# Hybrid decoder trunk with top-4-of-32 experts on one core: down products of the experts as three fp32r passes instead of fp32 matmuls

## The chip, the cores and the metric

One core of a Trainium2 chip. The metric is the device time of one launch in microseconds, the median over runs of the same program; besides there is one profiled execution, whose own time stands in the table below.

## The reference

One layer for 1024 prompt tokens and 32 sample tokens (8 sequences of 4), model width 1024, all in fp32: conditioning and RMSNorm, an input projection, a recurrent head group (HGRN2) and a pooling group, an output projection with a residual, then the experts, a residual and a last RMSNorm. The change lies in the experts alone:

```python
def moe(h, w_router, b_router, w_gu, b_gu, w_down, b_down):   # top 4 of 32 experts, D_FF = 1024
    ...
    gu = lax.ragged_dot(xs, w_gu, group_sizes) + b_gu[e_sorted]
    gate = jnp.minimum(gu[:, :D_FF], SWIGLU_LIMIT)
    up = jnp.clip(gu[:, D_FF:], -SWIGLU_LIMIT, SWIGLU_LIMIT)
    act = gate * jax.nn.sigmoid(SWIGLU_ALPHA * gate) * (up + 1.0)
    out = lax.ragged_dot(act.astype(w_down.dtype), w_down, group_sizes) + b_down[e_sorted]
    out = out * probs.reshape(-1)[order][:, None].astype(out.dtype)
    y = jax.ops.segment_sum(out, tok_sorted, num_segments=n)
```

## The kernel before, in words

Four phases follow one another: `modulation`, `mixing` (with the router), `experts` and `combination`. The span spends 882 to 2496 us in `experts`, and only this function changes.

**Items.** The router leaves a table of items. An item is one expert with up to 128 of its tokens, and an item "with a tail" has up to 32 more (`TAIL`). Class 0 is plain, class 1 has a tail, class 2 is idle; `per_class` (L1398) walks the table on each engine in groups of eight and branches into `item(i, False)` or `item(i, True)`. Each item loads its expert's 12 MB anew.

**Weights.** SP loads an item's weights as 12 chunks of 1 MB into `raw0` to `raw11`: eight of gate and up (`KT` = 8 blocks of 128 rows of the model width, gate and up side by side) and four of down (`DN`, two blocks of 128 rows each). `reload` (L1433) waits until TensorE has used a chunk for the last time, by counting on `gu_done` (one per grain) or `dn_done` (one per pair of down blocks), and loads the next item's into the same place, in the order 0 to 11.

**Gate and up.** A grain is half of a gate-and-up chunk, 128 x 1024 numbers, 16 grains an item in the order of `ORDER`: first both halves of blocks 0 to 3, then the left halves of blocks 4 to 7, then the right ones. ACT rounds each grain to fp32r (`split_hi`, L1640), DVE subtracts that from the original (`split_lo`, L1708), into a ring of eight buffers `hi` and `lo` (`RING` = 8). TensorE computes hi x hi, hi x lo and lo x hi with the gathered rows, which are split in the same way (`xs`, by `rows_hi` and `rows_lo`): six matmuls of 128 x 512 a grain (L1592 to L1595), into the banks `pg[u][b]` (u: gate or up, b: half of the columns). The bias comes first, as a matmul of a selecting matrix with the biases (L1578). A grain's buffers are free for grain q + 8 when `gu_done` has counted grain q.

**SwiGLU.** `swiglu(i, b)` (L1717) on DVE takes half b: gate (min), up (clip), then with ACT's sigmoid (`squash`, L1651) the product and `act1`. b = 0 may start when grains 0 to 11 are done, b = 1 after all 16.

**Down.** TensorE transposes each half of `act1` (`transpose_act`, L1522) into the bank `pt0`, ACT copies it to `aT` (`act_cols`, L1655), and the 16 down matmuls (L1529, 8 blocks x 2 halves of the output) run in fp32 straight from `raw8` to `raw11`. Between them TensorE transposes the second half of `act1` (before block 2) and the next item's gathered rows (`transpose_rows`: the first half ahead of the down stage, the second before block 3).

**Output.** ACT copies bank `py0` and DVE copies `py1` to `y` (L1692, L1773), and POOL scatters `y` with an add to the output rows in DRAM (L1502). Then POOL gathers the rows for the next item. `y_out` counts landings of the scatters.

**Tail.** In an item with a tail TensorE also runs the 32 rows in fp32 from the raw chunks: `tail_up` (32 matmuls with `TAILED` at grains 6 and 11) into `py0`, `swiglu_tail` on DVE, and `tail_down` (four matmuls of 128 x 256 for each of eight blocks) into the bank `pg[1][0]`, two blocks at a time ahead of down blocks 0, 2, 4 and 6. ACT copies that bank to `act1` (L1688), POOL scatters it (L1497). Each engine's order is written out in its own `item` (TensorE L1563, ACT L1659, DVE L1752, POOL L1484). ACT's order after `squash(i, 0)` is: three grains of the next item, `act_cols(0)`, `squash(1)`, `rows_hi(0)`, one grain, `act_cols(1)`, `rows_hi(1)`, four grains, the tail's copies, the copy of `y`. DVE's is the same with `lo`, and ends with `select` (the next item's selecting matrix) and its copy of `y`. Before each item's first copy and before its first sigmoid ACT loads a function table.

## Time and profile before

| | us |
|---|---|
| median of 3 runs | 2581.58 |
| lowest, highest | 2580.42, 2586.19 |
| the profiled execution, its own time | 2580.96 |
| its span, first to last instruction | 2579.4 |
| TensorE (PE) busy in the span | 2373.8 |
| DVE, ACT, POOL busy | 1391.8, 1117.1, 566.2 |

Busy times come from the profiled execution. Matmuls are pipelined: a matmul's recorded length runs into the next one, so the pace is read from start to start. An fp32 matmul stands in the trace as two records, an fp32r matmul as one.

### The profile page before, as it was taken

To read this page: it belongs to the slowest core of one execution; us is meant where nothing else is said; L and a number is where in the kernel's file an instruction comes from. 1 tells how busy PE (TensorE), PEld (TensorE's weight loads), DVE (VectorE), ACT (ScalarE), POOL (GpSimd) and SP (SyncE) were. 2 spreads that over 40 slices of the span, in tenths; PEclk is the share of its full clock that TensorE was granted. 3 is DMA by queue.
4 is the path that set the end of the run, shared out by engine and by line. 5 is a ranking of instruction groups with operands and counts; after the bars stand their busy time and mean duration, and the time that the engine had idled before them with its cause. 6 is when DMAs were issued, how large, how long until landed. Compare 5 with 4: busy or idle time off the path is not lost. (4 is left out here: it accounts for less than half of the span.)

```text
span 2579.4 us, 36293 instructions
## 1 busy us (share of the span) xinstructions
PE 2373.8 (92%) x11130; PEld 1553.7 (60%) x11131; DVE 1391.8 (54%) x1996; ACT 1117.1 (43%) x1443; POOL 566.2 (22%) x843
## 2 busy tenths in 40 slices
PE   8589999999986399999999999999999999999965
PEld 1177677777754256556567566766575666676641
DVE  0124554545333566556466666766565575766647
ACT  0023333333221345445455455555454554555532
POOL 0122333333211312112112121221121212121110
PEclk9799999999687699999999999999999999999985
DMA  8840000000020787778689889988797797999945
GB/s 307 330 173 34 33 33 33 27 14 23 29 66 12 290 320 286 264 277 318 251 313 344 312 319 371 343 317 313 293 335 301 258 362 277 350 343 368 350 161 222
DMA packets 142977, 604.43 MB, mean 234 GB/s; under 512 B 20129, under 2 KB 25262, under 8 KB 104470
## 3 DMA queue, kind: packets, MB, share of 16 engines
q1 hardware_dynamic: 120311, 551.51, 55.0%
q0 software_dynamic: 21968, 50.99, 8.1%
q10 hardware_dynamic: 662, 1.50, 0.2%
q8 instruction: 18, 0.29, 0.0%
q14 instruction: 18, 0.14, 0.0%
HBM read 561.82 MB, written 42.30 MB: 234 GB/s over the span
## 5 line engine op out<-in xcount | busy, mean ns | idle before, releaser
L1710 DVE TENSOR_TENSOR lo<-raw,hi 128x1024 fp32r<-128x1024 f32 x600 | 716.6, 1222 | 200.1 <-ACT hi L1645 173.2
L1645 ACT ACTIVATE hi<-raw 128x1024 fp32r<-128x1024 f32 x600 | 613.1, 1054 | 172.4 <-PE pg L1595 172.4
L1529 PE MATMUL py<-raw,aT 128*128 128x512 f32 x1184 | 537.9, 599 | 6.3 <-ACT aT L1657 6.3
L1592 PE MATMUL pg<-hi,xs 128*128 128x512 f32 x1184 | 467.3, 395 | 0.0
L1593 PE MATMUL pg<-lo,xs 128*128 128x512 f32 x1184 | 465.3, 393 | 0.0
L1595 PE MATMUL pg<-hi,xs 128*128 128x512 f32 x1184 | 367.3, 392 | 0.0
L1529 PEld LDWEIGHTS py<-raw,aT 128*128 128x128 f32 x1184 | 214.5, 190 | 250.2 <-issue 238.0
L1592 PEld LDWEIGHTS pg<-hi,xs 128*128 128x128 f32 x1184 | 222.9, 188 | 68.9 <-issue 20.1
L1595 PEld LDWEIGHTS pg<-hi,xs 128*128 128x128 f32 x1184 | 222.8, 188 | 49.2
L1593 PEld LDWEIGHTS pg<-lo,xs 128*128 128x128 f32 x1184 | 223.1, 188 | 47.4
L392 PE MATMUL X<-hT,w_in 128*128 128x128 f32 (+1 forms) x1728 | 223.8, 289 | 0.8 <-issue 0.8
L392 PEld LDWEIGHTS X<-hT,w_in 128*128 128x128 f32 x1728 | 219.2, 208 | 1.2 <-issue 1.2
L1502 POOL DMA_INDIRECT moe_rows<-y,now x37 | 61.3, 1657 | 631.3 <-DVE y L1773 631.3
L498 PE MATMUL X<-w_out,mixT 128*128 128x512 f32 (+1 forms) x288 | 130.8, 614 | 7.1 <-issue 6.8
L400 PE MATMUL X<-w_in,hT 128*128 128x512 f32 (+1 forms) x288 | 128.2, 604 | 6.1 <-ACT vx L637 6.1
L1714 DVE TENSOR_TENSOR xs<-pt,xs 128x512 fp32r<-128x512 f32 x76 | 52.2, 687 | 118.5 <-ACT xs L1649 118.5
L1497 POOL DMA_INDIRECT moe_rows<-actm,now_t x12 | 17.2, 1435 | 433.5 <-ACT actm L1688 433.5
L1657 ACT ACTIVATE aT<-pt 128x512 f32<-128x512 f32 x74 | 44.2, 598 | 150.5 <-PE pt L1525 150.5
L498 PEld LDWEIGHTS X<-w_out,mixT 128*128 128x128 f32 (+1 forms) x288 | 52.9, 186 | 79.7 <-issue 79.2
L1653 ACT ACTIVATE sigm<-gatem 128x512 f32<-128x512 f32 x74 | 46.5, 629 | 124.1 <-DVE gatem L1724 124.1
L1724 DVE TENSOR_SCALAR gatem<-pg 128x512 f32<-128x512 f32 x74 | 51.1, 690 | 87.3 <-PE pg L1595 83.2
L400 PEld LDWEIGHTS X<-w_in,hT 128*128 128x128 f32 (+1 forms) x288 | 52.5, 185 | 75.2 <-issue 68.3
(295 smaller groups left out, 2581.0 us busy)
## 6 DMA issues: line engine op xcount, KB each, us to landing
raw<-in_w_gu SPq DMA_DIRECT2D x300, 1024.0 KB, 7.3
raw<-in_w_down SPq DMA_DIRECT2D x148, 1024.0 KB, 6.9
wada<-in_w_ada SPq DMA_DIRECT2D x12, 2048.0 KB, 7.7
w_in<-in_w_in SPq DMA_DIRECT2D x5, 2048.0 KB, 14.1
moe_rows<-zero SPq DMA_DIRECT2D x9, 512.0 KB, 11.6
x<-in_x_prompt SPq DMA_DIRECT2D x8, 512.0 KB
w_out<-in_w_out SPq DMA_DIRECT2D x1, 4096.0 KB, 25.0
xr<-in_x_prompt SPq DMA_DIRECT2D x8, 512.0 KB, 3.7
```

Source lines behind the costliest of these rows:

```text
L392: last = pe.matmul(bank[:, m * T:(m + 1) * T], w_in[:, kt, first + m * P:first + (m + 1) * P], hT[:, kt * T:(kt + 1) * T], start=(kt == 0) ...
L400: last = pe.matmul(bank[0:T, :], hT[:, kt * T:(kt + 1) * T], w_in[:, kt, first:first + HW], start=(kt == 0), stop=(kt == KT - 1))
L498: last = pe.matmul(bank[0:T, :], mixT[:, kt * T:(kt + 1) * T], w_out[:, kt, n * 512:(n + 1) * 512], start=(kt == 0), stop=(kt == KT - 1))
L1502: pool.indirect_dma_start(scratch["acc"][:, :], bass.IndirectOffsetOnAxis(ap=now[:, 1:2], axis=0), y[:, :], None, compute_op=ALU.add).then ...
L1529: return pe.matmul(py[n][:, :], aT[:, kt, :], raw[KT + kt // 2][:, kt % 2, n * 512:(n + 1) * 512], start=(kt == 0), stop=(kt == KT - 1))
L1592: pe.matmul(pg[u][b][:, :], xs[:, kt, 0, :], wh[:, u, :], start=False, stop=False)
L1593: pe.matmul(pg[u][b][:, :], xs[:, kt, 0, :], wl[:, u, :], start=False, stop=False)
L1595: last = pe.matmul(pg[u][b][:, :], xs[:, kt, 1, :], wh[:, u, :], start=False, stop=(kt == KT - 1))
L1645: act.activation(hi[q % RING][:, :, :], grain(q), ACT.Copy).then_inc(s["hi"], 1)
L1710: dve.tensor_tensor(lo[q % RING][:, :, :], grain(q), hi[q % RING][:, :, :].bitcast(F32), ALU.subtract).then_inc(s["lo"], 1)
L1714: dve.tensor_tensor(xs[:, half * 4:half * 4 + 4, 1, :], pt[1][:, :].rearrange("p (k t) -> p k t", k=4), xs[:, half * 4:half * 4 + 4, 0, :] ...
L1724: dve.tensor_scalar(gate[:, :], pg[0][b][:, :], LIMIT, None, ALU.min).then_inc(s["gate"], 1)
```

## The change

- **Down in three passes.** `GRAINS` becomes 24: grain 16 + kt is down block kt, and ACT and DVE split these eight grains as they do those of gate and up. `aT` gets a second plane: ACT writes the rounded activations, a new `act_lo` on DVE writes the rest (reads the bank `pt0`). `down_hi` and `down_lo` issue six fp32r matmuls a block instead of two fp32 ones. All consumers count on one semaphore `used` (23 a item, and `y_mm1` as the 24th).
- **Orders.** ACT and DVE convert grains 8 to 18 ahead of the first swiglu, 19 and 20 behind it, `act_lo(0)` ahead of `swiglu(1)`, grains 21 and 22 ahead of the second half's copy and `act_lo(1)`, 23 behind the rows, then the next item's 0 to 7. `select` moves ahead of grain 23.
- **Output.** ACT copies both halves of y, last in its item. DVE copies none. y is `act1`.
- **Tail.** `tail_down` runs four blocks at a time ahead of down blocks 0 and 4, and `yt_mm` is signalled at the second. ACT copies the bank to `pair` (which also holds `gate` and `up`) ahead of the next item's eight grains.
- **Spark.** Each item on ACT begins with a Sigmoid of a single number.

```diff
-    GRAINS, RING = 2 * KT, 8
+    GU, GRAINS, RING = 2 * KT, 3 * KT, 8
...
-        gate, sig, up = (sb(n, [P, 512]) for n in ("gatem", "sigm", "upm"))
+        sig, pair = sb("sigm", [P, 512]), sb("pair", [P, FF])
+        gate, up = pair[:, 0:512], pair[:, 512:1024]
         act1 = sb("actm", [P, FF])
-        aT = sb("aT", [P, FT, P])
-        y = sb("y", [P, D])
+        aT = sb("aT", [P, FT, 2, P], F32R)
+        y = act1
...
+        def wait_used(eng, i, q):
+
+            if q < GRAINS - 1:
+                eng.wait_ge(s["used"], i * (GRAINS - 1) + q + 1)
+            else:
+                eng.wait_ge(s["y_mm1"], i + 1)
...
-            def down(i, kt, n):
-                return pe.matmul(py[n][:, :], aT[:, kt, :], raw[KT + kt // 2][:, kt % 2, n * 512:(n + 1) * 512],
-                                 start=(kt == 0), stop=(kt == KT - 1))
+            def down_hi(kt, n):
+                q = GU + kt
+                pe.matmul(py[n][:, :], aT[:, kt, 0, :], hi[q % RING][:, n, :], start=(kt == 0), stop=False)
+                pe.matmul(py[n][:, :], aT[:, kt, 0, :], lo[q % RING][:, n, :], start=False, stop=False)
+
+            def down_lo(kt, n):
+                return pe.matmul(py[n][:, :], aT[:, kt, 1, :], hi[(GU + kt) % RING][:, n, :], start=False, stop=(kt == KT - 1))
...
-                    if tail and kt % 2 == 0:
+                    if tail and kt % 4 == 0:
                         if kt == 0:
                             pe.wait_ge(s["aT_t"], i + 1)
-                        tail_down(kt)
-                        tail_down(kt + 1)
+                        for c in range(2):
+                            pe.wait_ge(s[f"raw{KT + kt // 2 + c}"], i * 16 + 16)
+                        for k in range(4):
+                            last = tail_down(kt + k)
+                        if kt:
+                            last.then_inc(s["yt_mm"], 1)
+                    pe.wait_ge(s["lo"], i * GRAINS + GU + kt + 1)
                     for n in range(2):
-                        last = down(i, kt, n)
-                    if kt % 2:
-                        last.then_inc(s["dn_done"], 1)
+                        down_hi(kt, n)
+                    if kt % 4 == 0:
+                        pe.wait_ge(s["alo"], i * 2 + kt // 4 + 1)
+                    for n in range(2):
+                        last = down_lo(kt, n)
+                    last.then_inc(s["used"], 1)
+                pe.wait_ge(s["lo"], i * GRAINS + GRAINS)
                 for n in range(2):
                     for kt in (KT - 2, KT - 1):
-                        last = down(i, kt, n)
+                        down_hi(kt, n)
+                        last = down_lo(kt, n)
+                        if n and kt == KT - 2:
+                            last.then_inc(s["used"], 1)
                     last.then_inc(s[f"y_mm{n}"], 1)
...
             def item(i, tail):
+                act.activation(spark[:, 1:2], spark[:, 0:1], ACT.Sigmoid)
...
-                for q in range(RING, GRAINS):
+                for q in range(RING, GU + 3):
                     split_hi(i, q)
...
                 squash(i, 0)
-                for q in range(3):
-                    split_hi(i, GRAINS + q)
+                for q in range(GU + 3, GU + 5):
+                    split_hi(i, q)
                 act_cols(i, 0)
...
                 squash(i, 1)
                 rows_hi(i + 1, 0)
-                split_hi(i, GRAINS + 3)
+                split_hi(i, GU + 5)
+                split_hi(i, GU + 6)
                 act_cols(i, 1)
                 rows_hi(i + 1, 1)
-                for q in range(4, RING):
-                    split_hi(i, GRAINS + q)
+                split_hi(i, GU + 7)
                 if tail:
                     act.wait_ge(s["yt_mm"], i + 1)
                     for n in range(4):
-                        last = act.activation(act1[0:TAIL, n * W:(n + 1) * W], pg[1][0][n * TAIL:(n + 1) * TAIL, 0:W], ACT.Copy)
+                        last = act.activation(pair[0:TAIL, n * W:(n + 1) * W], pg[1][0][n * TAIL:(n + 1) * TAIL, 0:W], ACT.Copy)
                     last.then_inc(s["y_t"], 1)
+                for q in range(RING):
+                    split_hi(i, GRAINS + q)
                 act.wait_ge(s["y_mm0"], i + 1)
                 act.wait_ge(s["y_out"], i * 32 + 32)
                 act.activation(y[:, 0:512], py[0][:, :], ACT.Copy).then_inc(s["y0"], 1)
-
+                act.wait_ge(s["y_mm1"], i + 1)
+                act.activation(y[:, 512:1024], py[1][:, :], ACT.Copy).then_inc(s["y1"], 1)
...
+            def act_lo(i, b):
+                dve.wait_ge(s["aT"], i * 2 + b + 1)
+                dve.tensor_tensor(aT[:, b * 4:b * 4 + 4, 1, :], pt[0][:, :].rearrange("p (k t) -> p k t", k=4),
+                                  aT[:, b * 4:b * 4 + 4, 0, :].bitcast(F32), ALU.subtract).then_inc(s["alo"], 1)
...
                 swiglu(i, 0)
-                for q in range(2):
-                    split_lo(i, GRAINS + q)
+                for q in range(GU + 3, GU + 5):
+                    split_lo(i, q)
+                act_lo(i, 0)
                 swiglu(i, 1)
                 rows_lo(i + 1, 0)
-                split_lo(i, GRAINS + 2)
-                split_lo(i, GRAINS + 3)
+                split_lo(i, GU + 5)
+                split_lo(i, GU + 6)
+                act_lo(i, 1)
                 rows_lo(i + 1, 1)
-                for q in range(4, RING):
+                select(i + 1)
+                split_lo(i, GU + 7)
+                for q in range(RING):
                     split_lo(i, GRAINS + q)
-                select(i + 1)
-                dve.wait_ge(s["y_mm1"], i + 1)
-                dve.wait_ge(s["y_out"], i * 32 + 32)
-                dve.tensor_copy(y[:, 512:1024], py[1][:, :]).then_inc(s["y1"], 1)
```

## Rows read from the trace of the kernel before

**Rows 1.** Stretches: length, each engine's busy us, granted clock, DMA share, GB/s.
```profile
1213.57:1266.69 53.12, 52.72 (x296) 30.82 (x294) 28.14 (x32) 25.23 (x32) 8.56 (x13) 1.00 0.74 276
1567.58:1606.53 38.95, 38.70 (x150) 26.52 (x149) 26.56 (x28) 22.66 (x25) 8.14 (x12) 1.00 0.93 352
```

**Rows 2.** Stretches again, POOL's busy us in the tail's scatter (L1497) alone.
```profile
976.33:1015.28 38.95, 0.85 (x1) 1.00 0.90 337
...
2183.57:2222.51 38.94, 0.85 (x1) 1.00 0.90 336
```

**Rows 3.** Groups: count | busy us, mean ns | idle before, releaser.
```profile
L1529 PE MATMUL py<-raw,aT 128*128 128x512 f32 x1184 | 537.9, 599 | 6.3 <-ACT aT L1657 6.3
...
L1502 POOL DMA_INDIRECT moe_rows<-y,now x37 | 61.3, 1657 | 631.3 <-DVE y L1773 631.3
...
L1645 ACT ACT_TABLE_LOAD x25 | 32.1, 1283 | 19.9 <-issue 19.9
...
L1497 POOL DMA_INDIRECT moe_rows<-actm,now_t x12 | 17.2, 1435 | 433.5 <-ACT actm L1688 433.5
```

**Rows 4.** PE in order of time, plain item: start us, us, line, tile, count.
```profile
1514.36 3.70 PE L1529 MATMUL py<-raw,aT 128*128 128x512 f32 x8 [0.25 <-ACT aT L1657]
1517.89 0.60 PE L1525 MATMUL pt<-ident,actm 128*128 128x128 f32 x4
1518.33 1.88 PE L1529 MATMUL py<-raw,aT 128*128 128x512 f32 x4
1520.05 0.60 PE L1519 MATMUL pt<-ident,xg 128*128 128x128 f32 x4
...
1528.67 1.02 PE L1578 MATMUL pg<-bgu,sel 128*128 128x512 f32 x2
1529.53 0.39 PE L1592 MATMUL pg<-hi,xs 128*128 128x512 f32 x1
...
1530.91 0.62 PE L1578 MATMUL pg<-bgu,sel 128*128 128x512 f32 x2
```

**Rows 5.** DVE in order of time, the same item.
```profile
1507.97 0.69 DVE L1724 TENSOR_SCALAR gatem<-pg 128x512 f32<-128x512 f32 x1 [3.37 <-PE pg L1595]
...
1510.24 0.69 DVE L1732 SCALAR_TENSOR_TENSOR actm<-upm,gatem 128x512 f32<-128x512 f32 x1
1510.85 2.35 DVE L1710 TENSOR_TENSOR lo<-raw,hi 128x1024 fp32r<-128x1024 f32 x2
...
1522.26 4.63 DVE L1710 TENSOR_TENSOR lo<-raw,hi 128x1024 fp32r<-128x1024 f32 x4 [0.25 <-ACT hi L1645]
...
1529.27 0.69 DVE L1773 COPY y<-py 128x512 f32<-128x512 f32 x1 [2.25 <-PE py L1529]
```

**Rows 6.** ACT in order of time, the same item.
```profile
1520.69 0.60 ACT L1649 ACTIVATE xs<-pt 128x512 fp32r<-128x512 f32 x1 [1.56 <-PE pt L1519]
1521.18 3.88 ACT L1645 ACTIVATE hi<-raw 128x1024 fp32r<-128x1024 f32 x4
...
1529.03 1.28 ACT L1645 ACT_TABLE_LOAD   x1 [0.79 <-issue]
1531.11 1.06 ACT L1645 ACTIVATE hi<-raw 128x1024 fp32r<-128x1024 f32 x1 [0.80 <-PE pg L1595]
```

**Rows 7.** PE in order of time, an item with a tail.
```profile
1247.79 1.07 PE L1559 MATMUL pg<-raw,xs_t 128*32 128x256 f32 x16 [0.40 <-ACT xs_t L1677]
1248.79 3.70 PE L1529 MATMUL py<-raw,aT 128*128 128x512 f32 x8
...
1267.19 0.68 PE L1536 MATMUL pt<-ident,xg_t 32*128 32x32 f32 x8
```

**Rows 8.** ACT in order of time, the end of that item.
```profile
1263.69 1.54 ACT L1688 ACTIVATE actm<-pg 32x256 f32<-32x256 f32 x4 [3.00 <-PE pg L1559]
...
1267.88 1.28 ACT L1662 ACT_TABLE_LOAD   x1 [1.62 <-issue]
1269.17 0.38 ACT L1662 ACTIVATE xs_t<-pt 128x256 f32<-128x256 f32 x1
```

More of the change, by code:

```diff
@@ L1363, in experts @@
         idx = sb("idx", [P, 3], I32)
+        spark = sb("spark", [1, 2])
         nxt = sb("nxt", [P, 3], I32)
@@ L1408, in per_class, with chunk @@
                                 body(i, True)
+        def chunk(q):
+            return ORDER[q][0] if q < GU else KT + (q - GU) // 2
         def grain(q):
-            kt, b = ORDER[q % GRAINS]
-            return raw[kt][:, :, b * 512:(b + 1) * 512]
+            if q < GU:
+                return raw[chunk(q)][:, :, ORDER[q][1] * 512:(ORDER[q][1] + 1) * 512]
+            return raw[chunk(q)][:, q % 2, :].rearrange("p (u n) -> p u n", u=2)
+        def wait_used(eng, i, q):
[3 more added lines that the diff above has]
+                eng.wait_ge(s["y_mm1"], i + 1)
         @block.sync
@@ L1497, in item @@
                     pool.indirect_dma_start(scratch["acc"][:, :], bass.IndirectOffsetOnAxis(ap=now_t[0:TAIL, 1:2], axis=0),
-                                            act1[0:TAIL, :], None, compute_op=ALU.add).then_inc(s["y_out"], 16)
+                                            pair[0:TAIL, :], None, compute_op=ALU.add).then_inc(s["y_out"], 16)
                 pool.wait_ge(s["y0"], i + 2)
@@ L1640, in split_hi @@
             def split_hi(i, q):
-                kt, b = ORDER[q % GRAINS]
-                act.wait_ge(s[f"raw{kt}"], (i + q // GRAINS) * 16 + 16)
+                act.wait_ge(s[f"raw{chunk(q % GRAINS)}"], (i + q // GRAINS) * 16 + 16)
                 if q >= RING:
-                    act.wait_ge(s["gu_done"], i * GRAINS + q - RING + 1)
-                act.activation(hi[q % RING][:, :, :], grain(q), ACT.Copy).then_inc(s["hi"], 1)
+                    wait_used(act, i, q - RING)
+                act.activation(hi[q % RING][:, :, :], grain(q % GRAINS), ACT.Copy).then_inc(s["hi"], 1)
             def rows_hi(item, half):
@@ L1656, in act_cols @@
                 act.wait_ge(s["aT_ps"], i * 2 + b + 1)
-                act.activation(aT[:, b * 4:b * 4 + 4, :], pt[0][:, :].rearrange("p (k t) -> p k t", k=4), ACT.Copy).then_inc(s["aT"], 1)
+                act.activation(aT[:, b * 4:b * 4 + 4, 0, :], pt[0][:, :].rearrange("p (k t) -> p k t", k=4), ACT.Copy).then_inc(s["aT"], 1)
             def item(i, tail):
+                act.activation(spark[:, 1:2], spark[:, 0:1], ACT.Sigmoid)
                 if tail:
@@ L1692, in item @@
                 act.activation(y[:, 0:512], py[0][:, :], ACT.Copy).then_inc(s["y0"], 1)
+                act.wait_ge(s["y_mm1"], i + 1)
+                act.activation(y[:, 512:1024], py[1][:, :], ACT.Copy).then_inc(s["y1"], 1)
+            act.wait_ge(s["spark"], 1)
             act.sem_inc(s["y0"], 1)
@@ L1717, in swiglu @@
             def swiglu(i, b):
[L1718 removed]
+                wait_used(dve, i, (GU - 4 if b == 0 else GU) - 1)
                 if b:
@@ L1752, in item @@
             def item(i, tail):
-                for q in range(RING, GRAINS):
+                for q in range(RING, GU + 3):
                     split_lo(i, q)
```

21 lines of the change are left out of this document (7 added, 14 removed).

## The prediction

> **What bounds the kernel now.** I read the page first, for the share of each engine, then the stretches of the expert stage item by item, then the costliest groups, and last the order in time of one plain item and one item with a tail. TensorE is busy for 2373.8 of 2579.4 us, the others for little over half or less (table above). In a plain item it is busy 38.70 of 38.95 us, at the full granted clock of 1.00, while DVE has 26.56 and ACT 22.66 us and the DMA engines are busy for 0.93 of the time; an item with a tail takes 53.12 us [rows 1]. So each item is as long as TensorE's own list of matmuls, and the other engines follow. There are 37 items (scatters of y) and 12 of them have a tail (scatters of the tail, [rows 3]); 24 are plain, and the first one is plain and starts behind the router; 8 of the 24 plain ones follow a tail (their stretch begins with the rest of the tail's scatter; first and last of the 8 in [rows 2]), 16 follow a plain one.
>
> What the reader is to see in the plain item: the down stage goes from 1514.36 to 1528.67 [rows 4]. The bias pair that follows holds 0.86 us up to grain 0, though six matmuls of a grain take only 1.38 us with the next bias pair at 1530.91, 0.23 us each; so two need 0.46, and the down stage really ends 0.40 us later, at 1529.07. It takes 14.71 us: 32 records (two per fp32 matmul, x1184 in [rows 3] over 37 items), two groups of four transposes at 0.44 us (1517.89 to 1518.33), and 0.1 us at the start. That is 0.43 us a record, 0.86 us a matmul, 13.73 us for the 16.
>
> **TensorE's part of the change.** Each fp32 down matmul becomes three fp32r ones of the kind that grains of gate and up use: 3 x 0.23 = 0.69 us in place of 0.86. Eight chunks of six matmuls take 8 x 1.38 = 11.04 us instead of 13.73: 2.69 us less per item if nothing waits. By the Trainium skill (TensorE: Matmul & The Clock Gate, section "Wait — 56ns, not 53.3ns?") warm matmuls of 512 columns start 215.7 ns apart, which as an estimate makes three of them 0.65 us and the gain about 0.76 us an item larger; the rows show 0.23 us for this kernel's pattern, so the page's value is not used.
>
> Items with a tail: from the first tail_down to the end 1247.79 to 1267.19, plus the same 0.40, is 19.80 us [rows 7]. Known parts: 4 x 1.0 for eight tail_downs (1247.79 to 1248.79), 13.73, and 0.88 for transposes, 18.61; the other 1.19 lie in the nine changes from one kind of matmul to another, 0.13 each. After: 4.0 + 11.04 + 0.88 + five changes x 0.13 = 16.57. That is 3.2 us less.
>
> **A new wait in plain items.** act_lo(0), a 128x512 operation out of PSUM like the gate's 0.69 us [rows 5], stands on DVE ahead of swiglu(1), and swiglu(1) is what transpose_act(1) waits for. Call A the start of act_lo(0), which is when TensorE starts the down stage. The next DVE operation begins 0.60 us on (1510.24, 0.69 long, next at 1510.85); swiglu takes 2.96 us from its gate to the end of act (1507.97 to 1510.93): transpose_act(1) at A + 3.65 with 0.1 to pick it up. TensorE has done two chunks by A + 2.8, so it stands for 0.8 us. Then 0.44, one chunk, 0.44 and five chunks: end at A + 3.65 + 0.88 + 6 x 1.38 = A + 12.81, against 14.71 before: 1.90 us less, not 2.69. The wait for act_lo(0) itself costs nothing, four matmuls of chunk 0 (0.92 us) cover it. With a tail, four tail_downs (2.0 us) lie ahead of chunk 0 and cover the whole of this wait.
>
> **Does the conversion keep up?** ACT and DVE now convert 24 grains instead of 16. The old items leave both idle; the new order leaves little. The chain around one plain item, from A:
> - rows transposes at 3.65 + 0.44 + 1.38 = 5.47; rows_hi(1) 0.64 later (1520.05 to 1520.69, [rows 4, 6]): 6.11. hi of grain 23 0.49 later: 6.60. Grains come 0.945 us apart (3.88 for four, one is 1.06 long, [rows 6]): the last of the eight for the next item, 31, starts at 14.16.
> - The two output copies, now both on ACT (DVE's copy of 0.69 is gone): starts at 15.11 and 15.6, end 16.2. A table load of 1.28, spark 0.2, next hi (grain 8) 17.75 to 18.8.
> - DVE: 11 grains at 1.14 (4.63 for four less 2.35 for two, [rows 5]), 12.5; swiglu(0) 2.88; two grains 2.3: next act_lo(0) at 36.5.
> TensorE's own ring gives end 12.81 plus what it needs from a real end to the next down stage, 38.94 - 14.71 = 24.23: 37.04. So TensorE stays the bound, with only 0.5 us to spare, and a plain item takes 37.04.
>
> Three unknowns lie in that chain. The spark is priced between 0 and 0.38 (the 256-column activation, [rows 8]); that one and the 512-column one of 0.60 differ by 0.22, which leaves about 0.2 without columns. The branch code between items left ACT idle 0.79 us before the load [rows 6]; I take nothing, because ACT's instruction stream would be ahead of its engine there, with the bound 0.79. The table load comes twice per plain item now, at the first copy (x25 in [rows 3]) and again at the sigmoid, which needs a set of its own. The spark asks for the Sigmoid set first, so I take one load; bound, two, 1.28 more.
> What follows a load: the row at 1269.17 starts 0.01 us after the load of 1267.88 ends [rows 8], so I take nothing more. The Trainium skill (ScalarE: Activation LUTs, section "What ACT_TABLE_LOAD costs") adds about 1380 ns of drain to the 1283 ns of the load. The trace agrees with the load and shows no such drain here.
>
> After a tail the chain is later: ACT copies the tail's output when the last tail_down is through, 0.13 us to pick up and 4 x 0.39 (1.54 for four, [rows 8]), and only then starts the eight grains: the last starts 1.68 + 6.62 = 8.3 after it, TensorE ends 4 x 1.38 + 0.13 = 5.65 after it. So hi 31 is at end + 2.65, the next act_lo(0) at end + 2.65 + (36.5 - 14.16) = end + 25.0 instead of 24.23. The item after a tail takes 37.8: 1.1 us less than before.
>
> **At no cost.** DVE's three grains more ahead of a tail's swiglu (3.4 us) are covered by the 20 fp32 tail_up matmuls that TensorE does before grain 11. The transfers: 0.93 x 38.95 = 36.2 us of DMA work per plain item, just under 37.04. SP's reloads follow the same matmuls as before, in the same order. Down chunks are now wanted eight grains (11 us) sooner, by ACT. The first of them is the ninth in SP's order; chunk 0 is released seven grains in (10.9 us with the biases), a chunk of 1.05 MB takes 3.0 us at the 352 GB/s of [rows 1], so it has landed at 38 us, and ACT wants it after the next item's grain 8, at 37 + 13. If that cover goes, the item is as long as the DMA work. POOL's scatter of y moves 2.5 us later, behind ACT's copies; swiglu(0) awaits its landing, 12 grains (16.5 us) into the item, and the gather queued behind it on POOL serves transposes 16 grains in. The tail's scatter moves earlier, since its copy no longer stands behind eight grains (7.6 us); TensorE's next item needs that bank, and it is copied 4 us before the item ends. y now shares act1, and gate and up share the tile that the tail's scatter reads; both are guarded by the same landing, so by the same 16.5 us. The clock: TensorE waits 0.25 us for aT [rows 4] and 0.40 us for aT_t [rows 7] now, and the granted clock stays at 1.00 [rows 1]; I take it that 0.8 us do not change that.
>
> **Sum.** 16 x 1.90 = 30.4; 8 x 1.1 = 8.8; 12 x 3.2 = 38.4; first item 1.9; the last output copy ends 16.2 - 12.81 = 3.4 us after TensorE instead of 0.9 (1529.96 less 1529.07), so -2.5. Together 77.0. The profiled execution took 2580.96 us (span 2579.4), which gives 2504.0; the median of the runs is 0.6 higher: 2504.6, say 2505.
>
> **Rivals.**
> 1. The conversion chain sets the pace (23%). A second table load (the spark does not do what it is for), or the 0.79 us of branches plus a dearer spark, add 1.3 to 1.4 us to a chain with 0.5 to spare: plain items 37.9, those after a tail 39.2. Sum 16 x 1.0 - 8 x 0.3 + 38.4 + 1.9 - 2.5 - 1.4 = 50: 2531. For it: the small margin, and DVE's sum of busy time. Against: the instruction stream can run ahead. The drain that the page on ScalarE states would give this same time of 2531.
> 2. TensorE does not wait (10%): every item gives its full 2.69 or 3.2, sum about 102, 2479. It needs swiglu(1) to come 0.8 us sooner than my order gives; its floor is the DMA work of 36.2, which it just touches.
> 3. Slower (5%): the transfers become the bound. Place: ACT's hi of a grain waits for its raw chunk. The engines are 0.93 busy, and the same 12 chunks plus gathers and an accumulating scatter must go through in a shorter item. It decides the sign where DMA work per plain item passes 40.5 us, because 24 x 1.6 eats the 38 of the tails; at 41 us the sum is 24 x 2.06 - 38.4 + 0.6 = +12: 2593. Against: bytes are the same, and 36.2 would have to grow by 12%.
> 4. Everything else, among it no change (2%).
>
> **How the numbers follow.** Forecast 60%, with 2495 to 2515 as its own range. The range goes from 2484, which holds part of the way to rival 2, to 2535, which holds rival 1; about 15% lies outside. Faster 0.93, within 0.2% (5 us, about what a measurement of this kernel can tell) 0.02, slower 0.05.
>
> **What would show it.** Plain items of 37.0 and items with a tail of 49.9; TensorE idle 0.8 us before transpose_act(1), put down to DVE's act; down matmuls 0.23 us apart; one table load per item, at the spark; ACT's next-item hi following the load at once. Wrong, if hi or lo of down grains wait for DMA, if act_lo(0) starts later than the copy of aT (the chain is then the bound), or if the granted clock leaves 1.00 in the expert stage.

## The result, and the profile after

The kernel after the change takes **2524.9 us** (median of 4 runs, 2524.7 to 2527.4) where the one before took 2581.8 on the same chip: a ratio of 0.978, with a 95% interval of 0.976 to 0.980 (the ratios below have theirs in brackets). The forecast case came true, inside the range, but 20 us above the predicted 2505. The profiled execution took 2524.7 us, its span is 2523.1. TensorE is busy for 2293.3 us, DVE for 1726.9 and ACT for 1364.2.

First the stretches, as in [rows 1]: length, each engine's busy us, granted clock, DMA share, GB/s. They are item 15, plain behind a plain one, and item 7, with a tail.

```profile
1544.61:1582.11 37.50, 36.71 (x165) 29.30 (x164) 35.49 (x38) 29.35 (x35) 11.60 (x12) 1.00 0.99 373
1205.17:1255.64 50.47, 49.86 (x311) 34.08 (x310) 36.81 (x41) 30.76 (x41) 11.23 (x13) 1.00 0.81 293
```

The plain item is 1.4 us shorter. TensorE (36.71 us busy), DVE (35.49) and the DMA queues (a share of 0.99) are now near its length of 37.50, and ACT has 29.35. Item lengths below are always from the start of an item's last down matmul to that of the next:

| us | before | predicted | after |
|---|---|---|---|
| plain after plain (16 items) | 38.93 | 37.04 | 37.51 |
| plain after a tail (8) | 38.93 | 37.8 | 37.74 |
| with a tail (11 of 12) | 53.12 | 49.9 | 50.48 |
| item 1, the first with a tail | 53.21 | 49.9 | 55.83 |
| first item (gain) | | 1.9 | 1.9 |
| end of the last item to the end of the span | 84.4 | 86.9 | 87.5 |

TensorE in order of time, end of item 15, after the change (start us, us, line, tile, count, idle before):

```profile
1566.28 0.63 PE L1610 MATMUL pg<-hi,xs 128*128 128x512 f32 x2
...
1567.68 0.63 PE L1610 MATMUL pg<-hi,xs 128*128 128x512 f32 x2
1568.14 0.60 PE L1536 MATMUL pt<-ident,actm 128*128 128x128 f32 x4
1568.58 0.60 PE L1530 MATMUL pt<-ident,xg 128*128 128x128 f32 x4
1569.51 0.49 PE L1541 MATMUL py<-hi,aT 128*128 128x512 f32 x1 [0.33 <-ACT aT L1677]
...
1571.94 0.62 PE L1545 MATMUL py<-hi,aT 128*128 128x512 f32 x2
1573.02 0.66 PE L1536 MATMUL pt<-ident,actm 128*128 128x128 f32 x4 [0.47 <-DVE actm L1758]
```

DVE in the same item, to be read beside [rows 5]:

```profile
1566.45 2.35 DVE L1736 TENSOR_TENSOR lo<-raw,hi 128x1024 fp32r<-128x1024 f32 x2
1569.41 0.69 DVE L1777 TENSOR_TENSOR aT<-pt,aT 128x512 fp32r<-128x512 f32 x1 [0.60 <-ACT aT L1677]
1570.02 0.68 DVE L1750 TENSOR_SCALAR pair<-pg 128x512 f32<-128x512 f32 x1
...
1572.28 0.69 DVE L1758 SCALAR_TENSOR_TENSOR actm<-pair 128x512 f32<-128x512 f32 x1
```

The new wait is where it was foretold: two chunks of the down stage, then TensorE stands until DVE has written the second half of act, 3.61 us behind the start of `act_lo(0)` (1569.41 to 1573.02; predicted 3.65). DVE had to wait 0.60 us for the copy of aT, so after a plain item the conversion chain (ACT's rounding and DVE's subtracting, one grain behind the other) is not the bound. ACT at the end of the item and over its border, beside [rows 6]:

```profile
1576.05 8.63 ACT L1665 ACTIVATE hi<-raw 128x1024 fp32r<-128x1024 f32 x9
1584.58 0.58 ACT L1715 ACTIVATE actm<-py 128x512 f32<-128x512 f32 x1
1585.05 0.59 ACT L1717 ACTIVATE actm<-py 128x512 f32<-128x512 f32 x1
1585.66 1.28 ACT L1680 ACT_TABLE_LOAD   x1
1586.96 0.20 ACT L1680 ACTIVATE spark<-spark 1x1 f32<-1x1 f32 x1
1587.07 1.04 ACT L1665 ACTIVATE hi<-raw 128x1024 fp32r<-128x1024 f32 x1
```

No gap for branches ahead of the load, none behind it, and a spark of 0.20 us: the three unknowns of the chain came out at their chosen values. The groups have one load at the spark per item, 37 in all.

### The profile page after: what moved, and what is told of

Read it like the earlier page. It is cut to its first block and busy times, and to the rows that moved or that the text cites. A ratio compares the mean times of both kernels' runs of the same rounds, so it can differ in the third digit from the quotient of the medians.

```text
span 2523.1 us, 38969 instructions
## 1 busy us (share of the span) xinstructions
PE 2293.3 (91%) x11722; PEld 1665.6 (66%) x11723; DVE 1726.9 (68%) x2330; ACT 1364.2 (54%) x1776; POOL 666.7 (26%) x843
## 5 line engine op out<-in xcount | busy, mean ns | idle before, releaser
L1736 DVE TENSOR_TENSOR lo<-raw,hi 128x1024 fp32r<-128x1024 f32 x896 | 1039.4, 1218 | 123.1 <-ACT hi L1665 121.3
L1665 ACT ACTIVATE hi<-raw 128x1024 fp32r<-128x1024 f32 x896 | 887.0, 1049 | 103.9 <-PE pg L1610 103.5
L1541 PE MATMUL py<-hi,aT 128*128 128x512 f32 x592 | 244.6, 413 | 8.2 <-ACT aT L1677 7.8
L1513 POOL DMA_INDIRECT moe_rows<-actm,now x37 | 88.7, 2398 | 585.3 <-ACT actm L1717 585.3
L1542 PE MATMUL py<-lo,aT 128*128 128x512 f32 x592 | 233.9, 395 | 0.0
L1545 PE MATMUL py<-hi,aT 128*128 128x512 f32 x592 | 197.7, 394 | 0.0
L1541 PEld LDWEIGHTS py<-hi,aT 128*128 128x128 f32 x592 | 111.1, 188 | 45.0 <-issue 18.3
L1545 PEld LDWEIGHTS py<-hi,aT 128*128 128x128 f32 x592 | 110.7, 187 | 27.3
L1542 PEld LDWEIGHTS py<-lo,aT 128*128 128x128 f32 x592 | 111.4, 188 | 21.3
L1673 ACT ACTIVATE sigm<-pair 128x512 f32<-128x512 f32 x74 | 46.8, 632 | 125.5 <-DVE pair L1750 125.5
L1508 POOL DMA_INDIRECT moe_rows<-pair,now_t x12 | 17.2, 1435 | 346.2 <-ACT pair L1709 346.2
```

The lines of the kernel that those rows point to most:

```text
L1513: pool.indirect_dma_start(scratch["acc"][:, :], bass.IndirectOffsetOnAxis(ap=now[:, 1:2], axis=0), y[:, :], None, compute_op=ALU.add).then ...
L1541: pe.matmul(py[n][:, :], aT[:, kt, 0, :], hi[q % RING][:, n, :], start=(kt == 0), stop=False)
L1542: pe.matmul(py[n][:, :], aT[:, kt, 0, :], lo[q % RING][:, n, :], start=False, stop=False)
L1545: return pe.matmul(py[n][:, :], aT[:, kt, 1, :], hi[(GU + kt) % RING][:, n, :], start=False, stop=(kt == KT - 1))
L1665: act.activation(hi[q % RING][:, :, :], grain(q % GRAINS), ACT.Copy).then_inc(s["hi"], 1)
L1736: dve.tensor_tensor(lo[q % RING][:, :, :], grain(q % GRAINS), hi[q % RING][:, :, :].bitcast(F32), ALU.subtract).then_inc(s["lo"], 1)
```

## The experiments

### What slowed the matmuls

In the rows of TensorE above two grains are 1.40 us apart (1566.28, 1567.68). Before the change they were 1.37, as these two rows of the kernel before show, from the middle of an item:

```profile
1541.91 0.62 PE L1595 MATMUL pg<-hi,xs 128*128 128x512 f32 x2
1543.29 0.62 PE L1595 MATMUL pg<-hi,xs 128*128 128x512 f32 x2
```

Over all items an fp32r matmul of 512 columns takes 0.2292 us before and 0.2333 after, from start to start (the pace, below). With 148 of them an item (96 of the grains, four of the biases, 48 of the down stage) this makes 0.6 us: the excess of the tail items (50.48 over 49.9), and more than that of the plain ones (0.47), where the wait for act came out 0.18 shorter than reckoned. The pace is the same whether DVE and ACT are busy or not, and fp32 matmuls stay at 0.429 a record. What else had changed was the place of the operands in SBUF. Tiles are put one behind the other, and the 8 bytes of `spark` take up 32. `xs` lay at byte 202176 of each partition before and at 202208 after, an odd multiple of 64 before and of 32 after. `aT`, the stationary operand of the down matmuls, is at an odd multiple of 32 after, too. `hi` and `lo` lie at multiples of 128 in both.

**e1_spark64**: the changed kernel, with `spark` 64 bytes long, which puts `xs` and `aT` at multiples of 128.

```diff
-        spark = sb("spark", [1, 2])
+        spark = sb("spark", [1, 16])
```

> The changed kernel with one size altered: the tile spark has 16 numbers instead of 2, so that every tile allocated behind it (xs and aT among them, from which the stationary operand is loaded) lies 32 bytes further on and at a multiple of 64 again, as xs did before the change. In the changed kernel fp32r matmuls start 0.2333 us apart against 0.2292 in the kernel before, whether or not DVE and ACT are busy beside them. Theory 'placement': the pace goes back to 0.229, plain items after a plain one from 37.51 to 37.1, items with a tail from 50.48 to 50.0, items after a tail stay near 37.7 (ACT's chain), total about 2512. Rival 'load' (more conversions beside the matmuls, or a longer program, slow them): the pace stays 0.233 and the total 2525.

Measured: 2503.5 us, ratio 0.970 (0.969 to 0.971), and a pace of 0.227, better than the 0.229 expected; e8 below asks why. Items of 36.75 (plain behind plain), 37.70 (plain behind a tail) and 49.77 us (with a tail); item lengths are given in this order from here on. The grains are 1.36 apart (two rows of TensorE):

```profile
1553.88 0.62 PE L1610 MATMUL pg<-hi,xs 128*128 128x512 f32 x2
1555.24 0.62 PE L1610 MATMUL pg<-hi,xs 128*128 128x512 f32 x2
```

**e2_before_pad32**: the converse, the kernel before with `xs` pushed on by 32 bytes.

```diff
+        gap = sb("gap", [1, 2])
         nxt = sb("nxt", [P, 3], I32)
```

> The kernel before with an unused tile of 8 bytes in the place where the changed kernel has spark: xs lies 32 bytes on, at an odd multiple of 32; hi, lo and the raw chunks stay. Theory 'placement': the pace of fp32r matmuls goes from 0.2292 to 0.233; 96 of them and 4 bias matmuls an item, x 0.0041 = 0.4 us, x 37 = 15 us: about 2597. Rival 'load': nothing changes, 2582.

Measured: 2594.5 us, 1.005 (1.0035 to 1.006); plain items 39.31, items with a tail 53.49, pace 0.2333.

**e3_before_ring_pad32**: the kernel before with the rings `hi` and `lo` at odd multiples of 32 and `xs` not (64 bytes on, it is at a multiple of 128).

```diff
+        gap = sb("gap", [1, 2])
         hi = [sb(f"hi{j}"
...
+        gap2 = sb("gap2", [1, 2])
         table = sb("table", [1, (ITEMS + 2) * 3], I32)
```

> The kernel before with an unused tile of 8 bytes ahead of the ring hi and lo, and another behind it: the moving operands hi and lo lie 32 bytes on, at odd multiples of 32, and xs lies 64 bytes on, at a multiple of 64. Theory 'placement, of the stationary operand only': 2582, pace 0.229. 'Placement, of either operand': about 2597. 'Load': 2582 here and in the run with the pad ahead of xs.

Measured: 2595.8 us, 1.005 (1.004 to 1.007), items 39.31 and 53.47, pace 0.233. Either operand alone costs the whole of it.

**e8_before_pad64**: the kernel before with `xs` at a multiple of 128 (`gap` of 64 bytes).

> The kernel before with an unused tile of 64 bytes ahead of xs. In the kernel before xs lies at an odd multiple of 64, in the changed kernel with the 64-byte spark at a multiple of 128, and the pace is 0.229 in the one and 0.227 in the other. Theory 'multiples of 128 are better still': the pace goes to 0.227, 100 matmuls an item x 0.002 x 37 = 7 us: about 2574. Rival 'the pace of 0.227 came with something else': 2582.

Measured: 2572.7 us, 0.997 (0.996 to 0.998), items 38.74 and 52.93, pace 0.227.

So the change without the shift is seen twice: at odd multiples of 32 it takes 2594.5 to 2524.9, at multiples of 128 it takes 2572.7 to 2503.5, 69.6 and 69.2 us. In the kernel before, `xs` at an odd multiple of 32 instead of 64 costs 12.7 (2594.5 less 2581.8).

### The spark

**e4_no_spark**: the changed kernel without it.

```diff
-                act.activation(spark[:, 1:2], spark[:, 0:1], ACT.Sigmoid)
```

> The changed kernel without the spark (the Sigmoid of one number at the start of each item on ACT). If the spark saves a table load, ACT loads a table twice per item again: at the first copy, which delays the next item's grain 8 by nothing new (the load stands there either way, the spark's 0.2 us go), and again before squash(0), behind grain 18, where ACT waits 1.9 us for DVE in a plain item anyway. Theory 'hidden': the second load fits in that wait, the total stays within 3 us of 2525, and items after a tail get 0.1 to 0.2 us shorter. Rival 'on the chain' (my rival 1 of the prediction): the load of 1.28 us delays squash(0), swiglu(0) and act_lo(0); with 0.6 us of slack at act_lo(0) in plain items and none after a tail, +0.5 us in 16 and +1.1 us in 8 items: 2540.

Measured: 2525.0 us, 0.978 (the same ratio as with it), items of 37.50, 37.67 and 50.48. Each plain item has two loads now, at its first copy and at the sigmoid (groups of ACT):

```profile
L1665 ACT ACT_TABLE_LOAD x25 | 32.1, 1283 | 0.4
L1673 ACT ACT_TABLE_LOAD x25 | 32.1, 1283 | 0.5
```

After a plain item the chain has the room for a second load; after a tail, where the chain is the bound, nothing is lost either. The spark is worth nothing here, and the second load of my rival 1 would not have cost what I gave it.

### The place of the tail's copies

**e6_tail_copy_late**: the changed kernel with ACT's copies of the tail's bank behind the next item's eight grains again, as before the change.

```diff
+                for q in range(RING):
+                    split_hi(i, GRAINS + q)
                 if tail:
                     act.wait_ge(s["yt_mm"], i + 1)
...
-                for q in range(RING):
-                    split_hi(i, GRAINS + q)
```

> The changed kernel with ACT's copies of the tail's bank put back behind the next item's eight hi grains. The last of these grains waits for y_mm1, the end of the down stage, so y_t comes after it: H31 + 0.95 + 1.55, with H31 starting 1.1 us sooner without the copies, at about the end + 1.1; TensorE's next bias waits for y_t. Theory 'TensorE waits': about 3.7 us at the start of each item after a tail, and a stretch of the low clock behind it where the wait is that long: 12 x 3.7 = 44 less what the next item gets back, total 2560 to 2575. Rival 'hidden': 2525.

Measured: 2581.3 us, 1.000 (0.999 to 1.001). The twelve items behind a tail grow from 37.7 to 42.7 and from 50.5 to 54.6 us on average, and of the others only item 1 does, by 0.7. That is more than the 2560 to 2575 us expected. TensorE at the border of items 8 and 9, and the stretches from that border (columns as above):

```profile
1327.20 0.39 PE L1545 MATMUL py<-hi,aT 128*128 128x512 f32 x1
1330.92 0.71 PE L1593 MATMUL pg<-bgu,sel 128*128 128x512 f32 x2 [3.32 <-issue]
...
1334.20 0.63 PE L1607 MATMUL pg<-hi,xs 128*128 128x512 f32 x1
1334.62 0.63 PE L1608 MATMUL pg<-lo,xs 128*128 128x512 f32 x1
```
```profile
1327.40:1331.00 3.60, 0.28 (x2) 0.12 (x2) 3.10 (x3) 3.54 (x8) 0.00 (x0) 1.00 1.01 398
1331.00:1340.00 9.00, 9.00 (x33) 7.15 (x34) 3.50 (x3) 5.88 (x7) 6.03 (x5) 0.81 0.79 184
```

and ACT:

```profile
1326.93 2.00 ACT L1665 ACTIVATE hi<-raw 128x1024 fp32r<-128x1024 f32 x2 [1.04 <-PE py L1545]
1328.85 1.52 ACT L1711 ACTIVATE pair<-pg 32x256 f32<-32x256 f32 x4
```

The bank is the next item's first one for `up`; it is free at 1330.37 (1328.85 + 1.52), and TensorE had been done since 1327.4. Its next matmul starts 0.55 us after that. The profile names no releaser, so that the bank is the cause rests on this edit. The wait has a second part: behind it the granted clock is 0.81 on average over 9 us, and the matmuls are 0.42 apart for a while instead of 0.23. With three passes instead of fp32, and the copies where they were, the kernel is no faster than before: the place of the copies is as much a part of the gain as the passes. The prediction had this right but at no more than a clause ("copied 4 us before the item ends").

### The shared y, and POOL

**e7_y1_on_dve**: the changed kernel, with the second copy of y back on DVE, behind its eight grains.

```diff
-                act.wait_ge(s["y_mm1"], i + 1)
-                act.activation(y[:, 512:1024], py[1][:, :], ACT.Copy).then_inc(s["y1"], 1)
...
                 for q in range(RING):
                     split_lo(i, GRAINS + q)
+                dve.wait_ge(s["y_mm1"], i + 1)
+                dve.wait_ge(s["y_out"], i * 32 + 32)
+                dve.tensor_copy(y[:, 512:1024], py[1][:, :]).then_inc(s["y1"], 1)
```

> The changed kernel with the copy of the second half of y back on DVE, behind the next item's eight lo grains and ahead of its grain 8. ACT's table load and grain 8 come 0.5 us sooner. DVE ends its eight grains 5.3 us into the item and starts grain 8 at 6.0 (plain) with a gap of 0.66, so the copy (0.69) replaces the gap. Theory 'DVE's sum is what counts after a tail': items after a tail keep 37.7 or gain up to 0.3, plain ones 37.5; total 2523 to 2526; the end of the kernel is later by up to 1 us. Rival 'ACT's chain counts': items after a tail 0.5 us shorter, total 2521.

Measured: 2629.2 us, 1.019 (1.017 to 1.020), far over what I expected. Plain items behind plain ones take 43.3 to 44.4 us. All others are as in the changed kernel or a little shorter (37.51 and 50.51), but for item 1 (56.75). The scatter is issued 6.8 us into an item instead of 4.4. In item 11 DVE and then POOL:

```profile
1392.45 10.39 DVE L1734 TENSOR_TENSOR lo<-raw,hi 128x1024 fp32r<-128x1024 f32 x9
1403.01 1.23 DVE L1734 TENSOR_TENSOR lo<-raw,hi 128x1024 fp32r<-128x1024 f32 x1 [0.17 <-ACT hi L1665]
...
1412.32 0.69 DVE L1748 TENSOR_SCALAR pair<-pg 128x512 f32<-128x512 f32 x1 [6.68 <-DMA moe_rows<-actm,now]
```
```profile
1393.39 9.77 POOL L1513 DMA_INDIRECT moe_rows<-actm,now  x1 [14.73 <-DVE actm L1806]
```

POOL's scatter instruction takes 9.77 us instead of 1.66 [rows 3], and ends at 1403.16, 0.3 us after DVE has paused for the first time (1402.84). One subtraction earlier, at 1401.61, DVE had begun 1.22 us behind the one before instead of 1.135; POOL ends 1.55 us behind that. `swiglu(0)` waits for the landing, because y is `act1` now.

**e5_reorder**: e1 with an order that does away with the wait of the down stage: `swiglu(1)` ahead of `act_lo(0)`, the two passes with `aT`'s first plane for blocks 0 to 3, both transposes, then the third passes; the second half is transposed into the free bank `pg[0][1]`.

```diff
                     for n in range(2):
                         down_hi(kt, n)
-                    if kt % 4 == 0:
+                    if kt < 3:
+                        continue
+                    if kt == 3:
+                        transpose_act(i, 1)
+                        transpose_rows(i + 1, 1)
+                    if kt <= 4:
                         pe.wait_ge(s["alo"], i * 2 + kt // 4 + 1)
...
+                    for k in range(4) if kt == 3 else (kt,):
...
-                act_lo(i, 0)
                 swiglu(i, 1)
+                act_lo(i, 0)
```

> The changed kernel with the 64-byte spark and another order around the down stage: DVE runs swiglu(1) ahead of act_lo(0); TensorE runs the hi and lo passes of down blocks 0 to 3 first (16 matmuls), then transpose_act(1) and the second transposes of rows, then the four blocks' third passes; the second half's transposes go to the bank pg[0][1], which is free by then. Theory 'the wait for act is a stall that the order makes': TensorE's idle time ahead of transpose_act(1) (0.5 us between records, 13.5 in all in the changed kernel) goes. In plain items after a plain one the conversion chain of ACT and DVE is then the bound at 36.4 (it was 36.75), after a tail 36.2 to 36.5 (it was 37.7), because swiglu(1) and with it the whole of DVE's list no longer stands behind the copy of aT; total about 2486. Rival 'the conversion chain was the bound everywhere already': no more than 3 us under the 2503 of the run with the 64-byte spark.

Measured: 2542.9 us, 0.986 (0.984 to 0.987), though most items got shorter: 36.01, 36.94 and 49.71. Five plain items, each the second behind a tail, took 45 to 48.6. The waits of DVE say where (waited for: us in total, times, longest):

```profile
DVE pair L1752 <- DMA moe_rows<-actm,now: 52.9, 5, 11.9
```

POOL in item 10, one of the five, and DVE over the same time:

```profile
1340.07 16.16 POOL L1513 DMA_INDIRECT moe_rows<-actm,now  x1 [16.88 <-ACT actm L1719]
```
```profile
1333.03 21.66 DVE L1738 TENSOR_TENSOR lo<-raw,hi 128x1024 fp32r<-128x1024 f32 x19
1366.59 0.69 DVE L1752 TENSOR_SCALAR pair<-pg 128x512 f32<-128x512 f32 x1 [11.90 <-DMA moe_rows<-actm,now]
```

DVE subtracts 19 times without a pause, until 1354.69, and POOL's instruction ends at 1356.23. (Three more scatters took 10.5 us in items with a tail, which did not get longer.) In item 11, where DVE has a pause of 0.65 us at 1389.7, it took 2.54 us. Two theories were left: DVE's unbroken run holds POOL up, or the scatter comes at a bad time for the queues, which at 36 us an item have no rest. Four kernels on this:

**e9_y_early** and **e10_reorder_y_early**: e1 and e5 with ACT's two copies of y ahead of its last three grains, so that the scatter is issued sooner: 1.9 us into a plain item instead of 4.5 in e1 and 4.1 in e5.

```diff
-                for q in range(RING):
+                for q in range(RING - 3):
                     split_hi(i, GRAINS + q)
...
                 act.activation(y[:, 512:1024], py[1][:, :], ACT.Copy).then_inc(s["y1"], 1)
+                for q in range(RING - 3, RING):
+                    split_hi(i, GRAINS + q)
```

> The kernel with spark at 64 bytes (2503.5 us), with ACT's two copies of y placed ahead of the last three hi grains (after the copies of grains 24 to 28) instead of behind all of them. The scatter is then issued about two grains (2.7 us) sooner. If the scatter's landing is hidden in that kernel, the 36 inner items do not change (36.75, 37.7 and 49.8 us) and only the last item gains, by at most 2.7 us: 2500.5 to 2503.5. If the three last hi copies, pushed back by the y copies (some 1.9 us), reach TensorE's first matmuls of the next item, items get longer by up to 1 us each and the kernel gets slower than 2503.5.

Measured: 2501.2 us, 0.969 (0.968 to 0.971), items as in e1: only the end of the kernel gained (88.0 us behind the last item's last down matmul in e1, 84.2 here). POOL and DVE in item 11 hold something against the first theory in its plain form:

```profile
1371.48 10.30 DVE L1738 TENSOR_TENSOR lo<-raw,hi 128x1024 fp32r<-128x1024 f32 x9
```
```profile
1378.14 1.78 POOL L1513 DMA_INDIRECT moe_rows<-actm,now  x1 [20.21 <-ACT actm L1717]
```

Here POOL's instruction takes 1.78 us in the middle of nine subtractions without a pause, and so it does in 25 of the 37 items.

> The reordered kernel (2542.9 us, whose five plain items of 45 to 48.6 us come with scatters that land 15 to 26 us after issue), with the same early copies of y. Theory one: the scatter's work on POOL is held up by DVE's unbroken run of subtractions, so issued 2.7 us sooner it gets through ahead of that run; landings fall back to 7 or 8 us, no item is over 40 us, items are 36.0, 36.9 and 49.7 us, and the kernel takes about 2483 us. Theory two: the queues fall behind because items of 36.0 us are shorter than the transfers of an item need; then the time of the scatter's issue does not matter, the five long items stay, and the kernel takes about 2540 us.

Measured: **2486.5 us**, 0.963 (0.962 to 0.9645), with no item over 37 among the plain ones: 36.0 mostly, 36.95 and 49.71. That is the best of all kernels here, 38 us below the one after the change. POOL in item 11, and DVE:

```profile
1374.50 5.66 POOL L1513 DMA_INDIRECT moe_rows<-actm,now  x1 [14.80 <-ACT actm L1719]
```
```profile
1369.44 9.16 DVE L1740 TENSOR_TENSOR lo<-raw,hi 128x1024 fp32r<-128x1024 f32 x8
1378.98 12.57 DVE L1740 TENSOR_TENSOR lo<-raw,hi 128x1024 fp32r<-128x1024 f32 x11 [0.37 <-ACT hi L1667]
```

The instruction is issued while DVE runs eight grains and gets through at the pause of 0.37 us ahead of the next eleven: not ahead of DVE's run, as expected, but in a break of it, and the landing takes about 11 us rather than 7 or 8. In item 10 of e5 there was no break for 14.6 us behind the issue.

**e11_reorder_dve_pause** and **e12_y1_dve_pause**: e5 and e7 with nothing sooner, but DVE waits at the head of an item until POOL is through.

```diff
                                         y[:, :], None, compute_op=ALU.add).then_inc(s["y_out"], 16 if tail else 32)
+                pool.engine_nop().then_inc(s["gone"], 1)
...
             def item(i, tail):
+                dve.wait_ge(s["gone"], i + 1)
                 for q in range(RING, GU + 3):
                     split_lo(i, q)
```

> The reordered kernel of 2542.9 us with its scatter as late as it was (issued 4.1 us into an item), but DVE waits at the head of each item until POOL is through its scatter instruction. In that kernel's item 10 the scatter instruction lasted 16.2 us and ended 1.5 us after a run of 17 subtractions on DVE had ended. Theory one, DVE's unbroken run holds POOL up: with the pause the instruction takes 1.7 to 3.7 us in every item, landings are 7 to 9 us after issue, DVE loses 0.2 to 2 us per item, plain items stay under 38 us, and the kernel takes 2485 to 2500 us although nothing is issued sooner. Theory two, the late issue itself is what collides (with SP's loads, or because the queues are behind): the pause changes nothing of that, the five plain items of 45 to 48.6 us stay, and the kernel takes 2540 us or more.

Measured: 2514.0 us, 0.974 (0.973 to 0.975), 29 us less than e5 though DVE was given a wait. No long items. The groups have POOL's scatter at 3154 ns on average instead of 5014 (count, busy us, mean ns, idle before):

```profile
L1513 POOL DMA_INDIRECT moe_rows<-actm,now x37 | 116.7, 3154 | 514.2 <-ACT actm L1720 514.2
```

The pause costs 1.71 us per item, within the 0.2 to 2 expected but at its upper end, and plain items take 37.33 rather than 36.0. The total is 14 us above the 2500 that I gave as the most, and 26 below the 2540 of the second theory.

> The kernel with the second copy of y back on DVE (2629.2 us, plain items after plain ones 43.3 to 44.4 us, the scatter instruction 9.8 us long), with the same wait of DVE for POOL at the head of each item. Theory one: the instruction falls to 2 or 3 us and the landing to 7 or 8 us after an issue at 6.8 us; DVE starts its eleven grains at 8.5 to 9.5 instead of 5.9 us and ends them at 21.5, so a plain item is 37.6 to 40 us and the kernel 2530 to 2570 us, faster than without the pause. Theory two (the late issue is the cost): plain items stay at 43 us or get 3 us longer, and the kernel takes 2629 us or more.

Measured: 2567.2 us, 0.995 (0.993 to 0.996), 62 us less than e7; plain items 39.0 and 39.9. POOL's group, and DVE in item 11:

```profile
L1513 POOL DMA_INDIRECT moe_rows<-actm,now x37 | 61.3, 1658 | 625.8 <-DVE actm L1809 625.8
```
```profile
1396.99 12.58 DVE L1736 TENSOR_TENSOR lo<-raw,hi 128x1024 fp32r<-128x1024 f32 x11 [2.70 <-POOLq L1515]
```

With DVE idle the instruction takes 1.66 us again, as before the change, and the landing comes 6.2 us after issue instead of 18.7. That settles it between the two theories: the issue comes as late as before, only DVE is held back, and both kernels get faster.

It does not settle when POOL is let in. In e7, e10 and most items of e5 the held instruction ends about 1.55 us behind the first break in DVE's run, and in e7 a subtraction that began 0.08 us late was break enough. But three scatters of e5 (15.0 us) ended only 0.4 us behind the first break, sooner than that, and the 25 of e9 and the 12 of items with a tail in e7 (1.8 to 2.1 us) were hardly held at all. The 25 of e9 came 0.96 to 1.01 us after a subtraction had started, the long ones of e7 0.94 to 0.96 after. So the moment of issue within a subtraction may decide; no run varies it alone, and it stays open.

The Trainium skill (SBUF — State Buffer, section "SBUF: two separate sides") states that DVE and GpSimd (POOL) share a port pair which is an "exclusive lock", held for a whole instruction. It counts a DVE instruction with two SBUF inputs among the holders only against a GpSimd instruction that reads SBUF, and it tells of transfers issued by GpSimd that starve, for want of descriptors, under DVE's 2-port modes. So the page names the two engines and would have been a reason to look where POOL issues; it does not plainly foresee this case, a scatter held up by subtractions of two SBUF tiles. The trace agrees that POOL is held up by DVE. That it is this port no run here shows. The page has the lock held for one instruction; in item 10 of e5 POOL was held over the 13 subtractions from 1340.07 to 1354.69, and in e9 it got in between two of them.

## Why the prediction was right, and where it was 20 us off

- **Likeliest case.** Right: TensorE stays the bound behind plain items, three passes are cheaper than fp32, and the wait for `transpose_act(1)` takes part of it back. In item 15 TensorE stands for 0.62 us: the last matmul of chunk 1 starts 0.23 behind 1571.94 and takes 0.23, the transposes start at 1573.02. I had reckoned 0.8. ("About 0.76 us an item larger" was a slip for 0.69; nothing in the sum used it.)
- **"Each fp32 down matmul becomes three fp32r ones ... 3 x 0.23".** This is the term that was mis-sized, and with it the unstated one that the gate and up matmuls cost what they did before. The pace went from 0.2292 to 0.2333 because eight bytes of `spark` moved the operands, in all fp32r matmuls of the item. The same shift cost the kernel before 12.7 us (e2). For the changed kernel no run has `xs` at an odd multiple of 64; e1's items are together about 19 us shorter for a pace better by 0.006, so 0.004 is worth some 13 us of the 20, as an estimate. With the operands at multiples of 128 (e1) the same code takes 2503.5, 1.5 us from the predicted number; that is partly luck, for the pace is then 0.227, better than the one I used, and it makes up for item 1. And 3 us of e1's gain lie ahead of the expert stage, where its code is that of the changed kernel (see the sum).
- **Item 1.** Missed: the first item with a tail is 5.3 us longer than its like, once. TensorE in order of time:

```profile
922.41 0.40 PE L1545 MATMUL py<-hi,aT 128*128 128x512 f32 x1
926.55 0.65 PE L1551 MATMUL pt<-ident,xg_t 32*128 32x32 f32 x8 [3.74 <-issue]
...
928.12 0.63 PE L1608 MATMUL pg<-lo,xs 128*128 128x512 f32 x1
928.54 0.63 PE L1607 MATMUL pg<-hi,xs 128*128 128x512 f32 x1
```

  A gap of 3.74 us "issue" at the first entry of the branch with a tail, and then matmuls 0.42 apart, with the clock granted at 0.63 of full speed between 926.5 and 931. The gap of 3.7 us, and the 1.7 us that matmuls lose in 3.4 us at half the clock, make up the 5.3. It is the one place in the expert stage of this kernel where the granted clock leaves 1.00. Code being loaded behind full DMA queues would be an explanation, but no run shows it: from 915 to 930 us the instruction queues move four packets in the changed kernel and three in the kernel before, which has no such gap. The cause stays open.
- **After a tail.** Right, 37.74 us on average against 37.8: `act_lo(0)` starts without idle time there, DVE and ACT are the bound. It is also why e1's faster matmuls gained nothing in these items (37.70).
- **The sum.** 16 x 0.47 + 11 x 0.58 + 5.9 (item 1, which the sum had as 49.9) is 19.8; the end costs 3.1 instead of 2.5, and the time ahead of the expert stage is 1.25 longer (first grain on TensorE at 884.62 instead of 883.37). That is no effect of the change as far as the runs show: over all kernels here, which are alike up to that stage, it comes between 881.6 and 885.0. Less the 0.5 that the items after a tail gave more, that is 21, the difference between a predicted gain of 77.0 and the span's 56.3.
- **Rival 1** (the conversion chain): did not hold behind plain items, and e4 shows that even its condition, a second table load, costs nothing. The first instruction behind the load starts 0.02 us after it, and the load 0.02 us after the copy ahead of it. The drain of about 1380 ns that the Trainium skill states (ScalarE: Activation LUTs, section "What ACT_TABLE_LOAD costs") does not show in this trace.
- **Rival 2** (no wait): the wait is there. e10 takes it away by another order, and only with the y copies moved; at 36.0 us an item it is where the DMA work of 36.2 was reckoned to be.
- **Rival 3** (the transfers): no grain waited for a chunk, with the queues at 0.99 busy.
- **"At no cost", POOL's scatter "2.5 us later".** The scatter moved 2.2 us in plain items (4.4 instead of 2.2 into the item) and was covered: in item 15 it landed by 1557.15, 6 us ahead of `swiglu(0)` at 1563.58. What I did not price is that its landing can grow when DVE is busy. The instruction grew from 1.66 to 2.40 us on average in the changed kernel, and with 2.4 us more delay (e7) it took 9.8 us in most plain items and the kernel 104 us more.
- **Slower, as a rival,** was looked for in the queues. The nearer mechanism, which the prediction does not have, was e7's and e5's: a scatter behind DVE's run, with y in `act1`.

## What to carry to other kernels

Before pricing a matmul by a row of the old trace, look whether the change moves any of its operands in SBUF: an unused tile of 8 bytes ahead of the operands cost the kernel before 0.5%, and 64 bytes instead of 8 gave the changed one 0.9%. When work is moved to DVE as long runs of two-input subtractions, look where POOL issues its transfers, and let a pause of DVE lie right behind each, as in e11 and e12, where every instruction then got through; who waits for their landing decides what a delay costs. A buffer that is shared to save space turns the landing of one transfer into a wait of the next item's first stage.

## What the hardware showed that I had not expected

- **Placement.** An fp32r matmul of 512 columns took 0.233 us with `xs` or the `hi` and `lo` rings at an odd multiple of 32 bytes, 0.229 with `xs` at an odd multiple of 64, 0.227 with both at multiples of 128. The Trainium skill's 215.7 ns (TensorE: Matmul & The Clock Gate, section "Wait — 56ns, not 53.3ns?") was reached by none of them. The fp32 matmuls did not move (0.429 a record). Why the place matters no run tells.
- **POOL behind DVE.** The same scatter instruction took 1.66 us with DVE idle, 2.4 on average in the changed kernel, up to 9.8 in e7 and up to 16.2 in e5, and 1.78 in the middle of DVE's run in e9; it landed 6.0 to 26.5 us after issue.
- **The clock.** After an idle time of 3.3 to 3.7 us of TensorE the granted clock fell from 1.00 to between 0.63 and 0.81 over the next 4.5 to 9 us, that is, to the lower of its two levels (1.2 GHz of 2.4) for part of that stretch; it made a wait of 3.3 us (e6) cost 5.
